# The sample's FFN of a hybrid decoder step: plain fp32 products replaced by three F32R products of split factors

## The reference

```python
def _conv_ffn(x, buf, w_up, b_up, w_conv, b_conv, w_down):
    h = jnp.einsum('btd,df->btf', x, w_up) + b_up
    full = jnp.concatenate([buf.astype(h.dtype), h], axis=1)   # two rows of state ahead
    hc = b_conv + full[:, 0:T] * w_conv[0]
    for j in range(1, CONV_WIDTH):                             # CONV_WIDTH = 3
        hc = hc + full[:, j:j + T] * w_conv[j]
    gate, val = hc[..., :D_FF], hc[..., D_FF:]                 # D_FF = 2816 = 22 x 128
    out = jnp.einsum('btf,fd->btd', jax.nn.gelu(gate) * val, w_down)
    return out, full[:, T:]
# x2 = LayerNorm(alpha * x1 + out)
```

## Time and profile before

| what | value |
|---|---|
| median of three runs | 3979.32 us |
| the profiled execution: its time, its span | 3989.43 us, 3987.5 us |
| granted TensorE clock, mean over the span | 0.919 |
| first product of the sample's FFN | 3764.03 us |
| end of its last up product | 3914.49 us |
| last down product ends, residual begins | 3973.90 us |
| PE, DVE, ACT, POOL busy over the whole span | 84%, 51%, 43%, 13% |

### The profile page before, as it was taken

One profiled execution on the slowest core, in us unless ns is written; L12 is line 12 of the kernel. 1 busy time (PEld: TensorE's weight loads), 2 busy tenths in 40 slices (PEclk: granted clock), 3 DMA queues, 4 the chain that ended last, 5 costly groups with the idle time before them and its releaser, 6 DMA issues. The chain is left out here.

```text
span 3987.5 us, 59417 instructions
## 1 busy us (share of the span) xinstructions
PE 3364.6 (84%) x20516; PEld 2632.2 (66%) x20516; DVE 2051.8 (51%) x3485; ACT 1715.5 (43%) x3432; POOL 529.1 (13%) x758
## 2 busy tenths in 40 slices
PE   6999833888888959897899998889988999998497
PEld 5999811767777846665666666666665766666293
DVE  2111164777774445555665556665556655557021
ACT  2111110666662123464455664455654456554031
POOL 0000000000003420011221110221112211122110
PEclk9999966999999979999999999999998999999557
DMA  3333345232204455466675667765657756564444
GB/s 138 113 109 116 99 132 161 57 77 66 72 1 153 148 191 176 168 229 233 245 241 193 220 216 256 257 229 176 235 178 265 268 197 216 182 238 175 141 152 154
DMA packets 318917, 685.43 MB, mean 172 GB/s; under 512 B 42839, under 2 KB 134903, under 8 KB 309631
## 3 DMA queue, kind: packets, MB, share of 16 engines
q1 hardware_dynamic: 268983, 519.48, 39.4%
q0 software_dynamic: 43840, 144.74, 10.4%
q10 hardware_dynamic: 5808, 17.57, 1.1%
HBM read 601.85 MB, written 80.44 MB: 171 GB/s over the span
## 5 line engine op out<-in xcount | busy, mean ns | idle before, releaser
L1875 DVE TENSOR_TENSOR F_w_lo<-F_raw,F_w_hi 128x512 fp32r<-128x512 f32 x704 | 497.4, 709 | 751.8 <-ACT F_w_hi L1771 750.6
L1634 PE MATMUL F_ps_u<-F_x_hi,F_w_hi 128*128 128x512 f32 x1408 | 593.5, 422 | 28.0 <-DVE F_x_lo L1881 28.0
L1771 ACT CAST F_w_hi<-F_raw 128x512 fp32r<-128x512 f32 x704 | 427.5, 615 | 396.4 <-PE F_ps_y L1636 210.7
L1635 PE MATMUL F_ps_u<-F_x_lo,F_w_hi 128*128 128x512 f32 x1408 | 562.6, 400 | 0.0
L1636 PE MATMUL F_ps_u<-F_x_hi,F_w_lo 128*128 128x512 f32 x1408 | 559.6, 397 | 0.0
L2055 POOL DMA_DIRECT2D F_vin<-cache_v x512 | 280.7, 548 | 1700.7 <-PE F_ps_d L1701 1632.7
L1634 PE MATMUL F_ps_y<-F_w_hi,F_g_hi 128*128 128x512 f32 x704 | 300.6, 427 | 73.7 <-DVE F_g_lo L1888 73.7
L1634 PEld LDWEIGHTS F_ps_u<-F_x_hi,F_w_hi 128*128 128x128 f32 x1408 | 271.3, 193 | 136.8 <-issue 85.0
L1929 DVE STREAM_TRANSPOSE F_kt<-F_kin 128x1024 f32<-128x1024 f32 x256 | 309.9, 1230 | 93.2 <-DMA F_kin<-cache_k 93.0
L1636 PEld LDWEIGHTS F_ps_u<-F_x_hi,F_w_lo 128*128 128x128 f32 x1408 | 270.6, 192 | 61.7
L1635 PEld LDWEIGHTS F_ps_u<-F_x_lo,F_w_hi 128*128 128x128 f32 x1408 | 272.1, 193 | 47.5
(11 more groups left out here) (281 smaller groups left out, 5972.5 us busy)
## 6 DMA issues: line engine op xcount, KB each, us to landing
F_kin<-cache_k SPq DMA_DIRECT2D x512, 256.0 KB, 3.8
F_vin<-cache_v POOLq DMA_DIRECT2D x512, 256.0 KB, 4.6
F_raw<-w_up_t SPq DMA_DIRECT2D x176, 512.0 KB, 6.0
F_raw<-w_down SPq DMA_DIRECT2D x176, 512.0 KB, 5.0
Fs_wu<-w_up_t SPq DMA_DIRECT2D x22, 1024.0 KB, 4.6
sc_qk<-A_qk SPq DMA_DIRECT2D x16, 1024.0 KB, 5.7
Fs_wd<-w_down SPq DMA_DIRECT2D x22, 512.0 KB, 3.2
A_prow<-w_in SPq DMA_DIRECT2D x8, 1028.0 KB, 4.8
```

The source lines that it names most:

```text
L1634: nc.tensor.matmul(out, a_hi, b_hi, start=first, stop=False)
L1635: nc.tensor.matmul(out, a_hi, b_lo, start=False, stop=False)
L1771: nc.scalar.copy(w_hi[:, q % 4, :], raw[:, unit % RAW, q % 2 * 512:(q % 2 + 1) * 512]).then_inc(hi_done, 1)
L1875: nc.vector.tensor_tensor(w_lo[:, q % 4, :], raw[:, q // 2 % RAW, q % 2 * 512:(q % 2 + 1) * 512], w_hi[:, q % 4, :].bitcast(F32), ALU.subt ...
```

## The change

The two factors of each product are split into `hi` and `lo` in F32R, and each product is made of three. Raw weights come in 33 blocks of 1 MB (22 of `w_up`, then 11 of `w_down`, each with all 1024 output columns) through one ring of three buffers, `raw`; a buffer is refilled when DVE has made the `lo` part of its block. ACT rounds a block with one copy of 128x2048 (`high`), DVE subtracts with one of 128x2048 (`low`), into two buffers each (`w_hi`, `w_lo`). The input `x` and the gated product `g` are split too. All coefficients come in one load at the start. The loops are written out, and DVE reads both halves of the output after the last product.

```diff
-        wu = m.sb("wu", [P, 2, 2, DC, P])
-        wd = m.sb("wd", [P, 2, WG, 512])
+        raw = m.sb("raw", [P, RAW, 2 * D])            # RAW = 3
+        w_hi, w_lo = m.sb("w_hi", [P, 2, 2 * D], F32R), m.sb("w_lo", [P, 2, 2 * D], F32R)
+        coef = m.sb("coef", [P, FC, 2, 5])
+        LOADS = FC + FC // 2
...
         def _(sp):
+            def load(n):
+                if n >= RAW:
+                    sp.wait_ge(lo_done, n - RAW + 1)
+                if n < FC:
+                    sp.dma_start(raw[:, n % RAW, :], io["w_up_t"][n].rearrange("p g c k -> p (g c k)")).then_inc(raw_in[n % RAW], 16)
+                else:
+                    f = 2 * (n - FC)
+                    sp.dma_start(raw[:, n % RAW, :].rearrange("p (a d) -> p a d", a=2),
+                                 io["w_down"][0, f * P:(f + 2) * P, :].rearrange("(a p) d -> p a d", p=P))\
+                        .then_inc(raw_in[n % RAW], 16)
+
+            sp.dma_start(x[:, :, :], sc["x1T"][TILES, :, :, 0:S]).then_inc(x_in, 16)
+            load(0)
+            sp.dma_start(coef[:, :, :, :], io["coef_t"].rearrange("f p g k -> p f g k")).then_inc(s_in, 16)
+            sp.dma_start(hist[:, :, :, :, :], io["state_conv_t"]).then_inc(s_in, 16)
+            load(1)
+            load(2)
...
         def _(pe):
+            pe.wait_ge(x_lo_done, 1)
+            for f in range(FC):
+                pe.wait_ge(lo_done, f + 1)
                 for gv in range(2):
-                    pe.wait_ge(up_out, 2 * f + gv + 1)
+                    if f >= 2:
+                        pe.wait_ge(up_out, 2 * (f - 2) + gv + 1)
                     for c in range(DC):
-                        last = nc.tensor.matmul(ps[:, par, gv, 0:N], wu[:, par, gv, c, :], xT[:, c, :],
-                                                start=c == 0, stop=c == DC - 1)
+                        nc.tensor.matmul(out, w_hi[:, f % 2, cols], x_hi[:, c, :], start=c == 0, stop=False)
+                        nc.tensor.matmul(out, w_hi[:, f % 2, cols], x_lo[:, c, :], start=False, stop=False)
+                        last = nc.tensor.matmul(out, w_lo[:, f % 2, cols], x_hi[:, c, :], start=False, stop=c == DC - 1)
+                last.then_inc(w_used, 1)
+            for n in range(FC, LOADS):
+                pe.wait_ge(lo_done, n + 1)
+                for a in range(2):
+                    f = 2 * (n - FC) + a
+                    pe.wait_ge(g_lo_done, f + 1)
+                    for half in range(2):
+                        nc.tensor.matmul(out, g_hi[:, f, :], w_hi[:, n % 2, cols], start=f == 0, stop=False)
+                        nc.tensor.matmul(out, g_hi[:, f, :], w_lo[:, n % 2, cols], start=False, stop=False)
+                        last = nc.tensor.matmul(out, g_lo[:, f, :], w_hi[:, n % 2, cols], start=False, stop=f == FC - 1)
+                last.then_inc(w_used, 1)
...
         def _(act):
+            def high(n):
+                act.wait_ge(raw_in[n % RAW], 16 * (n // RAW + 1))
+                if n >= 2:
+                    act.wait_ge(w_used, n - 1)
+                nc.scalar.copy(w_hi[:, n % 2, :], raw[:, n % RAW, :]).then_inc(hi_done, 1)
...
+            nc.scalar.copy(x_hi[:, :, :], x[:, :, :]).then_inc(x_hi_done, 1)
+            act.wait_ge(s_in, 32)
+            for n in range(2):
+                high(n)
+            for f in range(FC):
+                up_done(f)          # waits for w_used, f + 1; two bias copies as before
+                high(f + 2)
+                if f:
+                    gelu(f - 1)
+                if f >= 2:
+                    round_g(f - 2)
+            gelu(FC - 1)
+            round_g(FC - 2)
+            round_g(FC - 1)
+            for n in range(FC + 2, LOADS):
+                high(n)
...
         def _(dve):
+            def low(n):
+                dve.wait_ge(hi_done, n + 1)
+                nc.vector.tensor_tensor(w_lo[:, n % 2, :], raw[:, n % RAW, :], w_hi[:, n % 2, :].bitcast(F32), ALU.subtract)\
+                    .then_inc(lo_done, 1)
...
+            for f in range(FC):
+                conv(f)             # six taps, each but the last waits for the one before
+                low(f + 2)
+                if f:
+                    gate(f - 1)
+                if f >= 2:
+                    rest_of_g(f - 2)
...
+            dve.wait_ge(w_used, LOADS)
             for half in range(2):
-                dve.wait_ge(down_done, 2 + (half + 1) * (FC // WG))
```

## The result

The changed kernel takes 4047.76 us (median of 4 runs, 4043.2 to 4055.84), the kernel before 3983.15 us beside it (median of 4, 3978.43 to 3990.63). The ratio is 1.0163, with a 95% interval of 1.0144 to 1.0181: slower, by 57 to 72 us. Of the two profiled executions the spans are 4044.8 and 3987.5 us, 57.3 apart.

The account below looks back on a forecast made before the run. Bound: PE in the up phase (weight loads at clock 0.50), transfers in the down phase. Start +1.0, up +74.8, down -18.0, end +0.7 make +58.5 us on the median 3979.3: 4038, range 4026 to 4058 (about 8 in 10).

Parts of the forecast that it names:

- The start: Sample's FFN up to its first product: first product at 3765.0, 1.0 us more than before.
- The up phase: 1056 F32R products in 22 chunks of 10.24 us: 225.3 us, 74.8 more than before.
- a price per weight load of 256 cycles for both formats: Up phase: a 128x128 load takes about 0.213 us at the lower clock, fp32 and F32R alike; three loads against two.
- The step that decided the sign: Up phase: the clock stays at 0.50 because the 64 columns are the same, giving 58.5 us more in all.
- the first rival: Up phase: the clock rises to the upper level; phase 116.2 us, time 3929; chance 5%.
- Series of load and stream: Up phase: a 128-cycle load, then the column stream; 0.160 us per F32R product, phase 169.0, time 3982; chance 4%.
- the second rival: Up phase: load and stream run in series; phase 169.0 us, time 3982, no change; chance 4%.
- The down phase: 11 blocks of 1 MB after the up phase: 41.4 us against 59.4 before, 18.0 less.
- two buffers, 4.3 us of hand-over: Down phase: rounding waits for a block's products; 4.3 us hand-over plus 2.8 of products, for two blocks: 3.5 per block.
- the third rival: Down phase gains nothing: gaps keep the clock at 0.50 or transfers limit; 56.8 us, time 4053; chance 9%.
- The end: Residual, norm and store: DVE reads both halves after the last product, 0.7 us more, 14.3 us.
- The whole: All parts summed: span 4046.0 against 3987.5, 58.5 us more, time 4038.

Follow-up runs that it names:

- e1: Changed kernel with 128 instead of 64 moving columns in the up phase's F32R products: 4049.1 us (one run).
- e3: Changed kernel with stationary blocks of 128x64 instead of 128x128 in the up phase, leaving out half of the hidden channels: 3935.0 us (one run).
- e2: Changed kernel with 256 instead of 64 moving columns in the up phase's F32R products: 3956.2 us, ratio 0.9923 to the kernel before.
- e7: Changed kernel with three buffers each for w_hi and w_lo instead of two: 4034.8 us (one run).
- e4: Changed kernel with the up phase in plain fp32 from the raw blocks, down phase still split: 3969.6 us, ratio 0.9961 to the kernel before.
- e6: e4 with 128 instead of 64 moving columns in the up products: 3909.7 us, ratio 0.9794 to the kernel before.
- e9: e6 with the down phase in plain fp32 from the ring too, nothing split: 3902.8 us, ratio 0.9781 to the kernel before.

## Why the prediction was right

**The start** was taken at 3765.0 and came at 3762.6. The last transfer to land was the state's, near 3758.2, where I had the coefficients' near 3759, and the stage began 1.1 us sooner in this execution. The rest is my rounding up: 3759 and 4.2 make 3763.2, not 3764, and I took 3765.

**The up phase** was 225.3, as predicted to a tenth. The step that carried it, a price per weight load of 256 cycles for both formats, is shown by e1 and e3. The step that decided the sign, that the clock stays at 0.50, is seen in the profile after. My reason for it, the 64 streamed columns, is borne out by e2: with 256 columns and an equally busy PE the clock rose. The 1056 products then took 128.8 us for the phase and 3956 us in all, against the 3929 and 116.2 that I had given to the first rival. Of these 27 us, 12.6 are in the phase: the distance, 0.12 instead of 0.11, and the cold start. The down phase has 1.1 of them. The others lie outside of the stage, which began near 3755.5 instead of 3750.6, and in the 10.1 that I had taken off for the reference. e2 is not quite that rival, though. No run had 64 columns at clock 1.00, so whether their distance would be 0.11 or 0.12 stays open.

**Series of load and stream**, the second rival, fell already with the profile after (0.213 us apart, not 0.160), and again with e1 (0.213, not 0.267).

**The down phase** was given 41.4 and took 42.5. The account (two buffers, 4.3 us of hand-over) is confirmed by e7. In the traces a pair of blocks takes 7.4 us, 3.7 each against the 3.5 of the sum: from a block's first product to what waits for its last are 3.1 us (4027.33 to 4030.44 in the chain), not 2.8, since the last one's own latency counts. The first three blocks took 12.8 us where I had 13.1, the other eight 29.7 where I had 28.3. The clock was 0.96 and PE waited for `low` and for no transfer, so the third rival fell.

**The end** was 14.3 and measured 14.4.

**The whole**: a stage of 295.3 against 295.4. That it was met to a tenth is luck: the start was 1.3 us too long and the down phase 1.1 too short. The time is 4047.8 against 4038, inside the range but 10 us off, though the stage was met. No step of the stage is behind this: I put the difference onto the median of three runs, 3979.3, and with a fourth it was 3983.2, which is 3.8 of the 10. The other 6 lie ahead of the stage or in the spread of the runs: the medians are 64.6 us apart, the stages of the two profiled executions 58.4. The kernel before has run at 3983 to 3995 as a median since then, and the spread of its runs (3978 to 4007) is the real uncertainty of such a forecast.

## What to carry to other kernels

With few moving columns (64 or 128 here for F32R, at clock 0.50), count weight loads and not products. Splitting an fp32 product into three F32R ones is then three loads against two, and PE gains by it only where the stream is long enough to hide them, as with 512 columns. A PE that is 100% busy at clock 0.50 is a sign of that, and the remedy can be more columns, even ones that nobody reads, or, which was not tried here, the wide operand made the moving one. Before a transformation is judged by what it does to one phase, its parts should be separated: here all that came with the change but the split of the up phase (the ring with its larger blocks, the start without waiting for coefficients) was worth 24 us, and hid behind a loss of 82.

## What the runs showed that I had not expected

Adding useless columns to the up products made the kernel faster, by 95 us of stage for F32R (64 to 256 columns, changed kernel to e2) and by 59 for fp32 (64 to 128, e4 to e6). The effect was expected from the rows, but not that it beats all the rest of the change. With the clock at 1.00 the same loads of 128x128 come 0.112 us apart for fp32, instead of 0.213.

Plain fp32 with 512 columns and a stationary block of 64 columns runs at 0.435 us a record over the down phase of e9, so two records cost 0.87 us, where three F32R products cost 0.69 (3 x 0.23). F32R saves PE 0.18 us for each of the 44 products, some 8 us in all. With two buffers the hand-over, with ACT's 1.9 and DVE's 2.3 us for each block, costs more than that (42.9 us in e6 against 38.3 in e9). With three and a slow up phase ahead it does not (34.5 in e7). A ring of five with three buffers for the split down phase was not run.
